# Multiplying the first two weight slabs of a phase interleaved, tile by tile of the incoming activations

## What is computed

```python
for l in range(2):                                  # first block
    h = rms_norm(x, g_mix_norm[l]); z = h @ w_in[l]
    x = x + concat(norm(mla(z)), norm(sgu(z)), norm(pool(z))) @ w_out[l]        # phase "mix"
    h = rms_norm(x, g_ffn_norm[l])
    x = x + (silu(h @ w_gate[l]) * (h @ w_up[l])) @ w_down[l]                   # phase "ffn"
for i in range(2):                                  # second block
    hn = rmsnorm(h, norm_mix[i])
    h = h + (short_conv(hn) if i == 0 else dilated_attention(hn))               # "conv", "attn"
    h = h + squared_relu_mlp(rmsnorm(h, norm_mlp[i]))                           # "mlp"
    h = h + sigmoid(rmsnorm(h, norm_ple[i]) @ w_gate) * (p[i] @ w_proj)         # "ple"
return rmsnorm(h, norm_final)
```

## Time and profile before

| | |
|---|---|
| median of 3 runs | 2771.72 us (2771.29 to 2781.44) |
| profiled execution, its own time | 2774.78 us |
| its span, first to last instruction | 2773.0 us |
| mean granted TensorE clock | 0.974 of full speed |
| busy: PE / DVE / ACT / POOL | 95% / 54% / 17% / 53% |

### The profile page before, as it was taken

How to read it: one execution, slowest core, us unless ns; L and a number is a source line. 1 busy time by engine, 2 the same in 40 slices (tenths; PEclk the granted TensorE clock), 3 DMA queues, 4 the chain that set the end, 5 groups by cost and what they waited for, 6 DMA issues and landing times.

```text
span 2773.0 us, 30840 instructions
## 1 busy us (share of the span) xinstructions
PE 2633.6 (95%) x11906; PEld 2158.1 (78%) x11906; DVE 1505.1 (54%) x1678; ACT 471.5 (17%) x777; POOL 1475.7 (53%) x465
## 2 busy tenths in 40 slices
PE   7889999999899999999999999898999999999997
PEld 6658888877588888787878887687788878878875
DVE  5767454046675540457751715895379357815526
ACT  3342111022421110101100102200310042100012
POOL 4525665654266565555655655455336514656652
PEclk9899999998999999999999999999999999999998
DMA  4102223231022322232322222232112202222221
GB/s 148 61 16 96 101 91 105 92 112 62 2 105 91 106 91 96 87 104 84 108 77 105 91 98 94 75 106 76 61 46 91 106 32 81 94 78 104 91 97 54
DMA packets 36891, 236.70 MB, mean 85 GB/s; under 512 B 4048, under 2 KB 5584, under 8 KB 9168
## 3 DMA queue, kind: packets, MB, share of 16 engines
q1 hardware_dynamic: 33456, 230.78, 23.8%
q10 hardware_dynamic: 3360, 4.85, 0.6%
HBM read 233.51 MB, written 2.10 MB: 85 GB/s over the span
## 4 chain that ended last, share of the span: by engine, by line
PE 82%; DVE 11%; issue 3%; ACT 2%; DMA 1%; POOL 0%; DVEq 0%; ACTq 0%; SPq 0%; POOLq 0%
PE psum L440 25%; PE psum L441 25%; PE psum L442 25%; DVE work L1341 3%; PE psum L888 2%; DVE work L1265 2%; DVE x_low L1281 1%; PE psum L872 1%; PE psum L650 1%; DVE work L1338 1%; PE psum L897 1%; ACT mlp_high L999 1%; DVE x_res L1385 1%; PE psum L776 1%; PE psum L760 0%
## 5 line engine op out<-in xcount | busy, mean ns | idle before, releaser
L380 POOL TENSOR_SCALAR w_high<-w_stage 128x2048 fp32r<-128x2048 f32 x216 | 419.0, 1940 | 1242.1 <-PE psum L442 1230.3
L382 POOL TENSOR_TENSOR w_low<-w_stage,w_high 128x2048 fp32r<-128x2048 f32 x216 | 1026.1, 4751 | 18.0
L440 PE MATMUL psum<-x_high,w_high 128*128 128x512 f32 x2048 | 808.0, 395 | 38.5 <-DVE x_low L1281 36.9
L441 PE MATMUL psum<-x_low,w_high 128*128 128x512 f32 x2048 | 801.6, 391 | 0.0
L442 PE MATMUL psum<-x_high,w_low 128*128 128x512 f32 x2048 | 801.6, 391 | 0.0
L440 PEld LDWEIGHTS psum<-x_high,w_high 128*128 128x128 f32 x2048 | 387.6, 189 | 124.1 <-issue 31.8
L441 PEld LDWEIGHTS psum<-x_low,w_high 128*128 128x128 f32 x2048 | 387.6, 189 | 83.2 <-issue 2.4
L442 PEld LDWEIGHTS psum<-x_high,w_low 128*128 128x128 f32 x2048 | 387.2, 189 | 81.2
L1305 DVE TENSOR_TENSOR x_res<-psum,x_res 128x512 f32<-128x512 f32 x64 | 46.9, 733 | 372.5 <-PE psum L442 372.5
L440 PE MATMUL psum<-mlp_high,w_high 128*128 (+1 forms) x576 | 227.8, 396 | 14.2 <-DVE work L1338 11.0
L441 PE MATMUL psum<-mlp_low,w_high 128*128 (+1 forms) x576 | 226.7, 394 | 0.0
(11 more groups left out here) (240 smaller groups left out, 3162.8 us busy)
## 6 DMA issues: line engine op xcount, KB each, us to landing
w_stage<-in_wstream SPq DMA_DIRECT2D x216, 1024.0 KB, 4.9
x_res<-in_x SPq DMA_DIRECT2D x2, 1024.0 KB, 11.8
out_x<-attn_out SPq DMA_DIRECT2D x8, 256.0 KB, 2.1
inv_count_sb<-in_inv_count ACTq DMA_DIRECT2D x2, 512.0 KB, 8.7
ple_proj<-in_p ACTq DMA_DIRECT2D x2, 512.0 KB, 3.7
v_tok<-in_mask ACTq DMA_DIRECT2D x1, 576.0 KB, 3.9
w_spat<-in_spatial ACTq DMA_DIRECT2D x2, 256.0 KB, 5.2
diag_sb<-in_diag ACTq DMA_DIRECT2D x2, 256.0 KB, 9.4
```

The lines of the kernel that those rows point to most:

```text
L380: pool.tensor_scalar(wh[:, s, :], stage[:, s, :], 1.0, 1.0, ALU.mult, ALU.mult).then_inc(high_written, 1)
L382: pool.tensor_tensor(wl[:, s, :], stage[:, s, :], wh[:, s, :].bitcast(F32), ALU.subtract) \
L440: pe.matmul(out, wa, ra, start=start, stop=False)
L441: pe.matmul(out, wa, rb, start=False, stop=False)
```

## The change

A table `OPENING` gives the order of 16 steps, each a pair (slab, k) of two triples. TensorE's `opening_slabs` walks through it in place of `first_slab` and `plain_slab(p, 1, ...)`: slab 0's k = 0, 1, 2, then in turn slab 1's k = 0, slab 0's k = 3, slab 1's k = 1, and so on to slab 0's k = 7, then `rms_sum`, then slab 1's k = 5, 6, 7. The waits stay what they were, at their new places: `slab_split` of slab 1 stands ahead of its k = 0, `x_low` ahead of each k of slab 0. Nothing else changes: not the number of instructions, nor the other engines' programs, nor "ple".

```diff
+OPENING = [(0, 0), (0, 1), (0, 2), (1, 0), (0, 3), (1, 1), (0, 4), (1, 2), (0, 5), (1, 3), (0, 6), (1, 4), (0, 7),
+           (1, 5), (1, 6), (1, 7)]
...
-            def first_slab(p, banks):
+            def opening_slabs(p):
 
                 s = p.slab
-                pe.wait_ge(slab_split, s + 1)
-                for m in range(2):
-                    take(p, banks[m])
-                for k in range(8):
-                    pe.wait_ge(x_low, 8 * p.norm + k + 1)
+                for second, k in OPENING:
+                    if k == 0:
+                        pe.wait_ge(slab_split, s + second + 1)
+                        for m in range(2):
+                            take(p, 2 * second + m)
+                    if not second:
+                        pe.wait_ge(x_low, 8 * p.norm + k + 1)
                     for m in range(2):
-                        last = triple(ps[:, banks[m], :], *blk(s % 2, 2 * k + m), xh[:, k, :], xl[:, k, :], k == 0, k == 7)
+                        last = triple(ps[:, 2 * second + m, :], *blk((s + second) % 2, 2 * k + m), xh[:, k, :], xl[:, k, :],
+                                      k == 0, k == 7)
                         if k == 7:
                             last.then_inc(tile_done if m == 0 else slab_done, 1)
-                rms_sum(p)
+                    if (second, k) == (0, 7):
+                        rms_sum(p)
...
                 if opening:
-                    first_slab(p, (0, 1))
-                    plain_slab(p, 1, (2, 3))
+                    opening_slabs(p)
                     done = 2
```

More of the change, by code:

```diff
@@ L590, in conv @@
             def conv(p):
-                first_slab(p, (0, 1))
-                for j in range(1, 6):
+                opening_slabs(p)
+                for j in range(2, 6):
                     plain_slab(p, j, (2 * (j % 3), 2 * (j % 3) + 1))
```

## The result

| | before | after |
|---|---|---|
| median of the runs | 2776.58 us (4 runs, 2771.29 to 2781.95) | 2837.97 us (4 runs, 2836.4 to 2839.2) |
| ratio | | 1.0227, 95% interval 1.0205 to 1.0249 |
| profiled execution, its span | 2773.0 us | 2837.4 us |
| mean granted TensorE clock | 0.974 | 0.965 |

The change makes the kernel 2.3% slower. The predicted time, 2839, is 1 us off, and the range, 2808 to 2862, holds it. That it is so near is luck in part: the terms are off by up to 2.5 us each, both ways. The two profiles are 64.4 us apart in span, for 67.2 forecast. The next table gives it by phase: how much the stretch from the first matmul of a phase to the first matmul of the next one grew from the profile of before to that of after (mix 0 and the last column count from the kernel's own first matmul, some 15 us into the span; the two "ple" lost 0.03 and 0.01).

What follows compares the result with a forecast made beforehand. TensorE, busy 95% of the span, was taken as the bound, so its waits count. Phase losses sum to 67.2 us on 2774.78, giving 2842; that execution is 3.1 above the median, so 2839 us, range 2808 to 2862.

Steps and rivals of the forecast that it cites:

- (a): Opening of ffn 0: slab 1's first step, fourth in a fixed order, makes TensorE wait 3.2 us for its split.
- (b): TensorE's low clock after a wait: 1.7 us lost behind 3.2 us, bounds 0 and 1.7; 2.8 behind 5 us and more.
- (c): Slab 2 in ffn: its split starts with slab 0's end, TensorE waits 2.1 us; each ffn loses 7.0, bounds 5.3 and 8.7.
- (d): Mix 1 and conv, which have a gap to fill: losses of 1.2 and 1.6 us, bounds of each -0.5 and 4.
- (e): Mix 0: sum 10.9 us later, angles contending with slab 3's split add 6.1; loss 17.0 us, bounds 8 and 19.
- (f): Each mlp: the sum's 11.8 us delay reaches the down product's wait whole through VectorE, plus 1.5; 13.3 us, bounds 7 and 17.
- (g): Attn: no wait for slab 1's split, sum 6.8 us later, VectorE decides; loss 6.8 us, bounds 0 and 11.
- a sign of being wrong: Mlp and attn: TensorE's later waits for VectorE (L1338, L1400) shrinking by the delay would show the forecast wrong.
- The reorder past a waiting step: Openings: ready steps of slab 0 pass slab 1's waiting step, so TensorE is not held; 15 us faster, 2757; chance 0.04.
- The second wait is not hidden: Concerns the rival with the early wait hidden, the late one not: eight times 2.1 us lost, 15 won, 2773; chance 0.04.
- The third rival: Only TensorE's own lateness counts: VectorE catches up in mlp and attn, angles don't contend; 45.5 us slower, 2817; chance 0.20.
- slip of a whole split: VectorE slips one more split, 4.9 us in each mlp and attn, and the second wait lowers the clock; 2860; chance 0.10.

Runs made afterwards that it cites:

- first-wait: Changed kernel, but slab 1's first step stays fourth, then the rest of slab 0, the sum, the rest of slab 1; 2799.6 us, 1.0094 of before.
- second-wait: Changed kernel, but slab 1's first step comes seventh, so its split is hidden; slab 0 still ends with the 13th step; 2819.9 us, 1.0154 of before.
- sum late: Order of before (slab 0 whole, then slab 1), only the sum of squares moved five steps later, behind slab 1's k = 4; 2804.21 us, 1.0108 of before.
- sum early: Changed order of steps, but the sum of squares moved ahead, behind slab 0's k = 3 (k = 5 in mix 1 and conv); 2816.21 us, 1.0145 of before.

## Why the prediction was right, and where not

*(a), (b), (c): ffn.* Right term for term: 3.01 for 3.2, 1.7 for 1.7, 1.97 for 2.1, the sum 11.7 us later, 7.2 for 7.0. The first-wait and second-wait runs show the parts by themselves, 4.9 and 2.3.

*(b), elsewhere.* The cost of the clock behind a wait of some 3 us was taken as one number, 1.7. It was 0.1 (mlp 0), 1.7 (ffn), 2.9 (mix 1, mlp 1). The bounds of 0 and 1.7 were too low at the top. It makes 1.2 of the 2.5 us by which mix 1 (d) missed; the other 1.3 are low clock behind the narrow sums, a stretch that the forecast does not price. Conv, where it was 1.7, lost 1.8 for 1.6.

*(e): mix 0.* Right in mechanism and nearly in size, 15.2 for 17.0. Late sum: 10.4 us for 10.9, and with the sum put back 4.3 of the 16.0 us at the narrow sums are left. Angles beside the split: they end 17.8 us after the sum, 18.3 forecast, and 12.0 when the split is held back. The difference is behind the narrow sums, where the clock differs from profile to profile: with the split held back the phase got 3.3 us shorter and not 6.1.

*(f): mlp.* The size is nearly right, 11.4 and 12.5 for 13.3. What held is the passage through VectorE: in the change its delay at the first drain, 11.8 and 14.6 us, is 11.3 and 13.1 at the last one, and the phase loses about that. (In mlp 0 the sum is 10.1 us later and not 11.8, since the first wait cost no clock; bank 0 is drained 10.4 us after it, 10.9 forecast, 8.8 before.)

Two steps failed. The first is where TensorE stands. The forecast asked what the late drain of bank 0 does to VectorE, and not what it does to TensorE, which has three steps, 5.0 us with the sum, to cover 10.4. So TensorE stands at slab 2, 5.33 and 5.27 us, and the wait in the down product is 4.90 as before. The second is the reason given for the passage, "VectorE does two tiles per split and can't catch up", with "VectorE is never idle there". It idles 0.92 us ahead of each `mlp_low` [0.92 <-ACT mlp_high L1002], and with no split beside it takes a tile every 3.0 us, two in 6 of a slab's 10.9. In "sum late" it made up 9.5 us of 11.6. So that the delay passed whole in the change was not forced by VectorE's load; it depends on where the splits fall, which the forecast did not work out. In that the near hit is luck.

*(g): attn.* 5.3 for 6.8. The same step failed in part: VectorE is 8.4 us late at its first drain and 5.3 at its last. The later wait did shrink, from 8.84 to 5.60, which the forecast had named as a sign of being wrong; the new wait of 6.01 us at slab 2 and its 2.0 us of clock were not foreseen.

*The rivals.* The reorder past a waiting step is out: the fourth step's wait stands in seven openings with ready steps behind it. The second wait is not hidden. The third rival, that VectorE catches up and the angles don't contend, is out for the change's mlp and angles and holds in part in attn; with 45.5 in all it is 19 us off. No slip of a whole split was seen, but a second fall of the clock was, in mlp and attn.

## What to carry to other kernels

Before a step is moved ahead of ready work, compare its data's time with its new place, not its old one: here a split of 7.3 us was covered by eight steps and is not by three. Then ask of the shortened stretch between two releases what must happen in it on every engine; the small operation at the head of another engine's program, free for as long as the cover was long, cost 9.3 of the 64.4 us. And in a loop where two engines pace each other, neither carry an initial delay through to its end nor write it off without looking at where they meet: two kernels with VectorE equally late at the start of mlp 0 ended 9.2 us apart. Find where each engine waits first.

## What was not expected of the hardware

*The clock after a short idle.* Waits of 3.01, 3.02, 3.07 and 3.23 us cost 1.7, 0.1, 2.9 and 2.9 us of low clock; in "sum early" 2.85 us cost 1.7 and 2.78 us cost 0.1; in "second wait" 1.89 us cost 1.7 and in the change 1.97 us 0.1. The length of the idle alone does not give the cost. The Trainium skill (TensorE: Matmul & The Clock Gate, section Why this matters for your kernels) advises against idle gaps between matmuls that are long enough to throw TensorE back to its half clock. The rows with 0.50 and 0.65 agree that a gap can do it. The row with 1.00 behind 3.02 us shows that a gap of that length need not, and the 1.7 us behind 1.89 that a much shorter one can.

*A meeting decides 7 us.* The same copies take 1.44 or 7.43 us in two executions of one program, and L1669 took 4.61 where L1674 took 0.43. The drain L1341, which reads one operand from PSUM and one from SBUF, took 0.68 us beside a split. The Trainium skill (SBUF — State Buffer, section Who interferes with whom) holds that copies and `tensor_scalar` can enter modes in which they contend with GpSimd for a shared port pair, and that outside these modes an instruction with at most one input in SBUF does not contend; these rows agree. A meeting of this kind moved mix 1 by 9.5 us between two profiles of one program, so a difference under some 10 us between two single profiles of this kernel says nothing until the phases are laid side by side.
